# Seven-product pairs: the order of one addition and one product in the first pair of each run

## The reference

```python
h = rmsnorm(x, g_norm)
a_u, a_v, a_z, b_q, b_k, b_v, b_gd, b_z, c_q, c_z, gl = split_proj(h, w_in)
out_a = a_u * s * silu(a_z)                 # gMLP, s: spatial mix of a_v
out_b = gla_out(o, gn_g, b_z)               # gated linear attention
out_c = cross_attn(c_q, mk, mv) * silu(c_z) # 4 heads of 256 into 256 memory rows
gates = sigmoid(gl + b_gate).reshape(T, 3, D)
proj  = einsum('btic,icd->btid', stack(out_a, out_b, out_c), w_branch)
x     = x + sum(gates * proj, axis=-2) @ w_out
y     = rmsnorm(x, g_final)
```

## Time and profile before

| | us |
|---|---|
| median of 3 runs | 841.9 (840.26 to 842.95) |
| profiled execution, its own time | 839.92 |
| its span, first to last instruction | 838.0 |
| TensorE busy | 827.2 |
| TensorE weight load busy | 804.9 |
| DVE busy | 513.9 |
| ACT busy | 412.5 |
| POOL busy | 68.0 |

### The profile page before, as it was taken

How to read it: one execution, slowest core, us unless ns; L and a number is a source line. 1 busy time by engine, 2 the same in 40 slices (tenths; PEclk the granted TensorE clock), 3 DMA queues, 4 the chain that set the end, 5 groups by cost and what they waited for, 6 DMA issues and landing times.

```text
span 838.0 us, 16432 instructions
## 1 busy us (share of the span) xinstructions
PE 827.2 (99%) x6779; PEld 804.9 (96%) x6779; DVE 513.9 (61%) x869; ACT 412.5 (49%) x712; POOL 68.0 (8%) x122
## 2 busy tenths in 40 slices
PE   9999999999999999999999999999999999999997
PEld 8999999999999999999999999999889999999995
DVE  6536533644546465467846799445678988755534
ACT  7534446346766642445442353333238877733424
POOL 1001000000000213101011211001110000000000
PEclk9999999999999999999999999999999999999999
DMA  9324743231142659732476963334573442362302
GB/s 309 99 77 166 256 160 102 90 109 56 63 133 83 200 170 319 266 102 74 154 248 224 347 207 107 108 101 152 185 267 102 151 128 75 101 226 91 112 2 102
DMA packets 87206, 126.21 MB, mean 151 GB/s; under 512 B 3114, under 2 KB 73816, under 8 KB 87136
## 3 DMA queue, kind: packets, MB, share of 16 engines
q1 hardware_dynamic: 73328, 76.58, 28.3%
q0 software_dynamic: 13712, 48.57, 16.6%
q10 hardware_dynamic: 96, 0.06, 0.0%
HBM read 112.98 MB, written 12.22 MB: 149 GB/s over the span
## 4 chain that ended last, share of the span: by engine, by line
PE 96%; DVE 2%; ACT 1%; issue 1%; ACTq 0%; DVEq 0%
PE mm L1392 50%; PE mm L1432 12%; PE mm L1349 6%; PE mm L1364 5%; PE mm L1338 3%; PE mm L1685 2%; PE mm L1767 2%; PE p L1323 1%; PE p L1325 1%; PE p L1324 1%; PE mm L1706 1%; PE mm L1705 1%; PE mm L1704 1%; PE p L1644 1%; PE p L1614 1%; PE mm L1822 1%
## 5 line engine op out<-in xcount | busy, mean ns | idle before, releaser
L1392 PE MATMUL mm<-h_lo,w_hi 128*128 128x260 f32 (+1 forms) x832 | 170.0, 285 | 0.0
L1901 DVE TENSOR_TENSOR w_lo<-raw,w_hi 128x1024 fp32r<-128x1024 f32 x106 | 128.9, 1220 | 62.9 <-ACT w_hi L668 61.9
L1392 PE MATMUL mm<-h_hi,w_hi 128*128 128x260 f32 (+1 forms) x832 | 167.4, 283 | 0.0
L1392 PE MATMUL mm<-h_hi,w_lo 128*128 128x260 f32 (+1 forms) x832 | 167.2, 282 | 0.0
L1392 PEld LDWEIGHTS mm<-h_lo,w_hi 128*128 128x128 f32 x832 | 128.1, 188 | 2.5 <-issue 2.4
L1392 PEld LDWEIGHTS mm<-h_hi,w_hi 128*128 128x128 f32 x832 | 128.1, 188 | 0.0
L1392 PEld LDWEIGHTS mm<-h_hi,w_lo 128*128 128x128 f32 x832 | 128.1, 188 | 0.0
L668 ACT ACTIVATE w_hi<-raw 128x1024 fp32r<-128x1024 f32 x106 | 110.5, 1052 | 16.0 <-DMA raw<-in_w_mem_kv_dram 5.8
L1392 PE MATMUL mm<-x_lo,w_hi 128*128 128x260 f32 (+1 forms) x320 | 70.4, 285 | 0.0
L1392 PE MATMUL mm<-x_hi,w_hi 128*128 128x260 f32 (+1 forms) x320 | 69.5, 282 | 0.0
L1392 PE MATMUL mm<-x_hi,w_lo 128*128 128x260 f32 (+1 forms) x320 | 69.4, 282 | 0.0
(11 more groups left out here) (470 smaller groups left out, 1965.8 us busy)
## 6 DMA issues: line engine op xcount, KB each, us to landing
raw<-in_w_in_dram SPq DMA_DIRECT2D x43, 1024.0 KB, 5.5
raw<-in_w_branch_dram SPq DMA_DIRECT2D x12, 1024.0 KB, 5.1
raw<-in_w_mem_kv_dram SPq DMA_DIRECT2D x8, 1024.0 KB, 5.5
gate<-in_cache_mem_k_dram POOLq DMA_DIRECT2D x16, 512.0 KB, 6.5
tok<-in_cache_mem_v_dram POOLq DMA_DIRECT2D x14, 512.0 KB, 5.7
tok<-in_state_gla_dram POOLq DMA_DIRECT2D x8, 512.0 KB, 7.7
out_dram<-tok POOLq DMA_DIRECT2D x8, 512.0 KB, 7.4
work<-scr_q POOLq DMA_DIRECT2D x8, 512.0 KB, 5.0
```

The lines of the kernel that those rows point to most:

```text
L1392: ins = MM(mm[:, j % 2, a, 0:c1 - c0], wp[:, j, k, :], xp[:, k, c0:c1], start=(k == 0 and wp is w_hi and xp is xl), stop=(k == KT - 1 and ...
L1901: V.tensor_tensor(w_lo[:, j], raw[:, j // 2, :, (j % 2) * P:(j % 2 + 1) * P], f32(w_hi[:, j]), ALU.subtract).then_inc(split_done, 1)
```

## The change

Nothing is computed differently, no instruction is added or taken away. Three orders change.

- DVE, first pair of run 0: `add_low(0)` stands ahead of `pair_sums(1)` instead of behind it.
- DVE, first pair of run 1: `add_low(4)` stands behind `pair_sums(5)` as before but ahead of `hooks("CZ", 0)`.
- PE, both runs: P4 of the first pair stands ahead of `hooks(name, 1)` instead of behind it. In run 0 that hook is empty on PE, so its order is unchanged there. In run 1 P4 of pair 4 now stands ahead of the 8 transposes of the softmax.

```diff
@@ TensorE, pairs(q)
                     product("P7", q)
+                    product("P4", q)
                     hooks(name, 1)
                 elif q == begin(q) + 1:
-                    product("P4", q - 1)
                     product("P3", q - 1)
                     product("P6", q)
@@ VectorE, pairs_product(q): run 0
                     last_lo(q)
                     gate_first(q)
+                    add_low(q)
                     pair_sums(q + 1)
...
                 hooks(name, 2 * p)
-                add_low(q)
+                if q > begin(q):
+                    add_low(q)
                 hooks(name, 2 * p + 1)
@@ VectorE, pairs(q): run 1
                         pair_ahead(q + 1, 0)
+                if q == begin(q):
+                    add_low(q)
                 hooks(name, 2 * p)
-                add_low(q)
+                if q > begin(q):
+                    add_low(q)
                 if q % 2 == 1:
                     att_out_lo(h)
```

## The result

The changed kernel takes 843.9 us, median of 6 runs (843.43 to 846.56), beside 840.4 for the kernel before in 6 runs (840.01 to 842.95). The ratio is 1.0039, with a 95% interval of 1.0027 to 1.0052: slower by 3.3 us by the ratio, by 3.5 us from median to median. Forecast: 844.8, within 842.5 to 846.4.

What follows compares the result with a forecast made beforehand. TensorE was taken as the bound, busy 827.2 of 838.0 us, with DVE deciding when products start. Run 0's +2.77 and run 1's +0.1 gave +2.9: 842.8 profiled, 844.8 on the median's scale, range 842.5 to 846.4.

Steps and rivals of the forecast that it cites:

- Run 0, 2.77: Run 0: sums behind the corner make DVE late, P5(1) waits for its bank; +2.77 us, bounds 2.3 to 3.2.
- the spacings of pair 2: Run 0, DVE from L1966 to gate_rest(0): uncovered chain timed like pair 2's weights, steps 1.39, 0.95, 1.87, 0.61 us.
- Rival B: P5(1) not held by gate_rest(0); run 0 costs only 0.3, run 1 keeps its 0.5; sum -0.2, 841.7 us; chance 0.17.
- Run 1, +0.1: Run 1: some 0.5 us won by P6(5), given back at the values product, then P4(5) 0.1 late; bounds -0.5 to +0.9.
- ACT's late L1021: Run 1, last_hi(5) on ACT: from 645.98 to about 646.85, making DVE's last_lo(5) 0.8 us late.
- P4(5)'s margin: Run 1: slack of 0.7 us before P4(5), taking most of DVE's 0.8 us lag and leaving 0.1.
- Two pairs on DVE waits for TensorE again, and the lag ends there: Run 1, after P4(5): DVE's remaining lag disappears two pairs on, so nothing is added to the 0.1 us.
- Rival C: Forecast's run 0 loss, plus ACT's late high part costing P4(5) the full 0.9 us in run 1; +3.7, 845.6; chance 0.13.
- The clock, nothing added: TensorE's 2.3 us wait would not lower its clock, so 0 added; a fall would cost 1.44 us per twelve-matmul product.
- The mark of 844.4: Whole kernel: time from which it counts as slower, about 0.3% or 2.5 us; chance of slower 0.58.

Runs made afterwards that it cites:

- the bank freed early: Changed kernel with gate_rest(0) moved on DVE ahead of A12 and the last sum of pair 1; 846.6 us, 1.0066 to the kernel before.
- Half the move: Changed kernel, but in run 0 only the second sum (L1966) goes behind the corner, L1965 stays ahead; 842.57 us, 1.0021 to the kernel before.
- run 0 alone: Kernel before with only the change's DVE order in run 0; run 1 as before on all engines; 844.77 us against 841.25, 1.0044.
- the changed kernel again: The changed kernel itself, unaltered, measured again with a second trace; 845.22 us against 840.19 for the kernel before, 1.0058.
- P4 ahead only: Kernel before with P4(4) ahead of the softmax transposes on TensorE in run 1, DVE as before; 843.62 us, 1.0030.
- run 1 alone: Kernel before with only the change's run 1 orders on DVE and TensorE, run 0 as before; 841.48 us against 841.25, 1.0002.
- The split ahead of the maximum: Kernel before with one DVE swap in run 1, last_lo(4) ahead of att_max(0); 840.14 us against 841.15, 0.9990.
- corner ahead only: Kernel before with the corner ahead of the softmax on DVE in run 1, TensorE's order as before; 840.83 us against 841.15, 1.0001.

## Why the prediction was right

**Run 0, 2.77: right, measured 2.76.** Each step is in the rows after. The corner didn't move. The sums came out of DVE's idle time, and the rest followed by the spacings of pair 2. P6(1) was 0.22 late at 396.09, forecast 0.31. P5(1) was held by L2008 and by nothing else: the bank freed early cuts the wait from 2.21 to 0.89. Half the move costs half. Rival B, that the bank doesn't hold, needed P5(1) before 398: it falls. The later L2008 lies 0.01 from its forecast (399.22 and 0.23 of start are 399.45, measured 399.44).

**Run 1, +0.1: the way was right to the values product, the size wrong behind it; measured +0.6.** What was won at the transposes, 0.42 at P6(5) against a forecast of 0.5, was given back at the values product to within 0.01. ACT's late L1021 was there, and DVE behind it 0.97 late (651.10 - 647.14 - 2.99), forecast 0.8. P4(5)'s margin took 0.7 of it, as worked out; 0.25 was left. The step that failed is "Two pairs on DVE waits for TensorE again, and the lag ends there". In the changed kernel DVE reaches the maximum of pair 6 late as well, ACT's first exponential comes at 666.77, 0.78 late, and the copy of P6, L1057, stands in ACT's queue behind it. P7(6) waits for that copy by the code, and starts 0.15 behind its end (667.23 + 0.38 = 667.61, to 667.76). It had a margin of 0.2 before, so 0.56 goes through. DVE did idle between, 0.91 ahead of L1955 of pair 6, but for ACT's L1021, and ACT there waited for a sum that DVE itself makes: the stretch is 0.91 in both kernels and took nothing of the lag. The link to P7(6) lies 20 us behind the edit, beyond the stretch that the prediction read; it is read off the traces, and no run takes it away by itself. Rival C was right that the lag gets through, but not on the place: it had all of it at P4(5), and 0.9.

**The clock, nothing added: wrong in part of the executions.** In the first trace it stayed at 1.00 and the sum came out; in the second trace of the same kernel, and in that of run 0 alone, it fell behind the same wait, for about 1.5 us. What the prediction had as the price of such a fall, 1.44 for twelve matmuls, is near it, though it takes 15 matmuls at 0.095 each and not 12 at 0.12. Its evidence was a row near the end of the program, where the stretch with TensorE idle still showed 1.00: one row can't exclude what happens in some executions. The fall may be part of the spread of the six runs, 843.43 to 846.56; only one of them has a trace. By the Trainium skill (TensorE: Matmul & The Clock Gate, HAM oscillation — how this bites in real kernels) idle gaps throw the array back to half clock; the gaps of its example are longer than these. Of the three traces with a 2.2 us wait at P5(1), two show such a fall and one does not.

**The sum.** 2.77 + 0.1 = 2.9 was forecast. In the profiled executions it was 2.76 + 0.63 + 0.23 of start = 3.62, and in the medians 3.5 (ratio 1.0039). The forecast of 844.8 against a measured 843.9 is high because the median of before, 841.9, lay in the upper cluster; with more runs it was 840.4. From 840.4 the same +2.9 gives 843.3. So that 844.8 lies near the measured time is in part luck: the change was taken 0.6 too small and the base 1.5 too high. On the scale of the profiled execution, 842.8 was forecast and 843.54 measured. The mark of 844.4, from which the prediction would have called the kernel slower, hung on the same base: 843.9 lies below it, and still the interval of the ratio leaves out 1.

## What to carry to other kernels

Work that lies in an engine's idle time ahead of a wait is free only there: move the wait in front of it, and all of it, with all that is queued behind, is paid. Ask first whether the instruction moved forward can start sooner at all; here its input came no earlier, so run 0's move had nothing to win. When an engine is late and never idles for long, follow the lag down each in-order queue that reads from it until an idle stretch as long as the lag has taken it up, not just to the next wait. Idle time counts for this only if what ends it doesn't hang on the late engine itself.

## What was not expected of the hardware

Behind a wait of 2.1 to 2.2 us of TensorE the granted clock falls to 0.50 in one execution and not in another of the same kernel. It fell in three of four profiled executions with such a wait (run 0 alone 2.22, the changed kernel again 2.23, P4 ahead only 2.13) and not in the fourth (2.21), nor behind the 1.91 of the bank freed early. In each it costs about 1.5 us. What decides isn't shown: the five runs of the changed kernel's second set lie within 0.44 of each other, so it may also be the chip or the occasion.

A fall of the clock at the start of the program may be what parts the clusters of the times. Busy time by stretch of the kernel before, whose profiled execution is of the faster cluster, and of run 1 alone, of the slower:

```profile
12.00:16.00 4.00, 4.00 (x32) 3.63 (x31) 4.00 (x7) 3.58 (x6) 0.00 (x0) 1.00 1.03 408
```

```profile
12.00:16.00 4.00, 4.00 (x24) 3.78 (x23) 3.38 (x7) 3.08 (x6) 0.00 (x0) 0.67 1.04 406
```

In the second TensorE waits 1.27 for a load at 7.88, the clock is 0.67 in these 4 us, and P4(0) starts 1.93 later (394.63 against 392.70). The trace of half of the move has the same, with a wait of 1.40 and P4(0) at 394.55. The split ahead of the maximum waits 1.11, its clock stays at 1.00, and P4(0) is at 393.17. So it fell behind the two longest of these waits, but the cause was not tried by itself, and the clock isn't all: in run 0 alone and in corner ahead only it is 1.00 there as well, and P4(0) still starts at 394.00 and 393.71. No trace of the kernel before from the slower cluster was taken.
